# Modulation vectors of a two-layer adaLN trunk: four column groups by block of output features, and one transpose

## The reference

```python
def modulated_norm(x, g, shift, scale):
    return rmsnorm(x, g) * (1 + scale[:, None]) + shift[:, None]

def trunk_layer(x, c, lw, token_mix):
    ...
    mod = (jax.nn.silu(c) @ w_ada + b_ada).reshape(c.shape[0], N_SUB, 3, D_MODEL)
    x = half_ffn(x, mod[:, 0], g_norm[0], w_ff_up[0], w_ff_down[0])
    h = modulated_norm(x, g_norm[1], mod[:, 1, 0], mod[:, 1, 1])
    ...
    x = half_ffn(x, mod[:, 2], g_norm[2], w_ff_up[1], w_ff_down[1])
```

## Time and profile before

| | |
|---|---|
| time, median of 3 runs | 3243.67 us (3242.27 to 3249.42) |
| span of the profiled execution | 3248.1 us |
| PE busy | 3163.6 us, 97% of the span |
| PE weight loads busy | 2826.5 us, 87% |
| DVE busy | 1155.2 us, 36% |
| ACT busy | 827.2 us, 25% |
| granted clock of PE, mean | 0.984 |
| moved from HBM | 373.62 MB |

### The profile page before, as it was taken

One profiled execution on the slowest core, in us unless ns is written; L12 is line 12 of the kernel. 1 busy time (PEld: TensorE's weight loads), 2 busy tenths in 40 slices (PEclk: granted clock), 3 DMA queues, 4 the chain that ended last, 5 costly groups with the idle time before them and its releaser, 6 DMA issues.

```text
span 3248.1 us, 54636 instructions
## 1 busy us (share of the span) xinstructions
PE 3163.6 (97%) x23756; PEld 2826.5 (87%) x23756; DVE 1155.2 (36%) x1941; ACT 827.2 (25%) x1221; POOL 138.7 (4%) x269
## 2 busy tenths in 40 slices
PE   8999999999999999999999999999999999999999
PEld 6999998867777899999999999987676778899999
DVE  3332334235332334333343323342444223343333
ACT  3221224232331122212222212242323211222121
POOL 0000000000411000000000000000003120000000
PEclk9999999989999999999999999998999999999999
DMA  5444432111258432333223444312022583322212
GB/s 241 145 173 154 157 131 88 66 39 49 82 172 273 135 118 83 136 146 110 89 75 134 165 169 146 129 53 91 27 75 63 189 275 99 127 79 85 96 71 77
DMA packets 118735, 390.85 MB, mean 120 GB/s; under 512 B 12784, under 2 KB 63312, under 8 KB 100320
## 3 DMA queue, kind: packets, MB, share of 16 engines
q1 hardware_dynamic: 100464, 338.36, 29.2%
q0 software_dynamic: 14432, 34.09, 3.1%
q10 hardware_dynamic: 3600, 14.91, 1.2%
HBM read 373.62 MB, written 13.69 MB: 119 GB/s over the span
## 4 chain that ended last, share of the span: by engine, by line
PE 87%; DMA 4%; DVE 3%; ACT 3%; issue 1%; SPq 1%; ACTq 0%; DVEq 0%
PE g L839 78%; PE q L839 5%; PE tb L839 4%; DMA w<-in_w_up 2%; DMA area<-in_w_ada 1%; ACT area L1749 1%; DMA area<-in_cache_v 1%; DVE w_lo L1949 1%; ACT area L1755 0%; SPq L703 0%; DVE w_rest L1907 0%; DVE area L2138 0%; ACT w_hi L1477 0%; DVE area L1876 0%; DMA area<-in_cache_k 0%
## 5 line engine op out<-in xcount | busy, mean ns | idle before, releaser
L839 PE MATMUL g<-h_hi,w_hi 128*128 128x272 f32 x2784 | 582.6, 290 | 16.9 <-ACT area L1486 9.7
L1477 ACT ACTIVATE w_hi<-w 128x1024 fp32r<-128x1024 f32 (+2 forms) x232 | 266.2, 1147 | 1259.5 <-PE g L839 939.0
L839 PE MATMUL g<-h_hi,w_lo 128*128 128x272 f32 x2784 | 577.6, 289 | 0.0
L839 PE MATMUL g<-h_lo,w_hi 128*128 128x272 f32 x2784 | 574.2, 287 | 0.0
L1949 DVE TENSOR_TENSOR w_lo<-w,w_hi 128x1024 fp32r<-128x1024 f32 (+2 forms) x232 | 309.9, 1336 | 512.7 <-ACT w_hi L1477 509.4
L839 PEld LDWEIGHTS g<-h_hi,w_hi 128*128 128x128 f32 x2784 | 438.4, 190 | 36.8 <-ACT area L1486 23.9
L839 PEld LDWEIGHTS g<-h_lo,w_hi 128*128 128x128 f32 x2784 | 437.3, 188 | 0.0
L839 PEld LDWEIGHTS g<-h_hi,w_lo 128*128 128x128 f32 x2784 | 436.6, 188 | 0.0
L839 PE MATMUL g<-h_hi,w_rest 128*128 128x272 f32 x1184 | 343.0, 292 | 0.0
L839 PE MATMUL g<-acts_hi,w_hi 128*128 128x272 f32 x1408 | 294.8, 290 | 0.0
L839 PE MATMUL g<-acts_hi,w_lo 128*128 128x272 f32 x1408 | 291.2, 288 | 0.0
(11 more groups left out here) (301 smaller groups left out, 4318.7 us busy)
## 6 DMA issues: line engine op xcount, KB each, us to landing
w<-in_w_up SPq DMA_DIRECT2D x44, 2048.0 KB, 7.9
w<-in_w_ada SPq DMA_DIRECT2D x32, 2048.0 KB, 7.7
w<-in_w_in SPq DMA_DIRECT2D x16, 2048.0 KB, 7.7
w<-in_w_down SPq DMA_DIRECT2D x16, 1536.0 KB, 6.5
w<-in_w_gate SPq DMA_DIRECT2D x48, 512.0 KB, 5.6
w<-in_w_down SPq DMA_DIRECT2D x16, 1280.0 KB, 5.5
area<-in_cache_k SPq DMA_DIRECT2D x72, 256.0 KB, 3.6
area<-in_cache_v SPq DMA_DIRECT2D x72, 256.0 KB, 4.3
```

The source lines that it names most:

```text
L839: return pe.matmul(o, a, b, start=start, stop=stop, skip_group_check=True, **kw)
L1477: ac.activation(WH[i % 2][:, 0:n], W[place][:, o:o + n], ACT.Copy).then_inc(s_wh, 1)
```

## The change

The four column groups take the four blocks of 128 output features, where they took blocks of the input. Each group sums over all eight `k` itself, and writes 128 columns. So a step issues 32 matmuls of 128 moving columns where it issued 8 of 512. The copy by ACT is 128 x 128. Rows are turned by one transpose of 128 x 128; the sum over groups and its constant `fold` fall away. DVE reads the first 9 of each 32 columns of `tb`.

```diff
-               seq_later=NS, fold=C, seq01=NS, own_seq=SEQS, new_mask=2 * NS, new_seq=2 * 4,
+               seq_later=NS, seq01=NS, own_seq=SEQS, new_mask=2 * NS, new_seq=2 * 4,
...
-        MR, _ = take(2, 4 * P, start=o_f + 6 * T)
-        CRAW, _ = take(KD, C, start=o_f + 6 * T + 8 * P)
+        MR, _ = take(2, P, start=o_f + 6 * T)
+        CRAW, _ = take(KD, C, start=o_f + 6 * T + 2 * P)
...
                 for k in range(KD):
-                    last = mm(Q[k % 4 * 32:k % 4 * 32 + 32, n % 2, :], COND[:, k, :], w[:, k * 512:(k + 1) * 512],
-                              k < 4, k >= 4)
+                    for j in range(4):
+                        o = k * 512 + j * P
+                        last = mm(Q[32 * j:32 * j + 32, n % 2, 0:P], COND[:, k, :], w[:, o:o + P], k == 0, k == KD - 1)
...
-                for b in range(4):
-                    last = mm(TB[:, n % 2, b * C:(b + 1) * C], MR[:, n % 2, b * P:(b + 1) * P], fold, True, True)
-                last.then_inc(s_feat, 1)
+                turn(TB[:, n % 2, 0:P], MR[:, n % 2, :], ident).then_inc(s_feat, 1)
...
-                ac.activation(MR[:, n % 2, :], Q[:, n % 2, :], ACT.Copy).then_inc(s_mr, 1)
+                ac.activation(MR[:, n % 2, :], Q[:, n % 2, 0:P], ACT.Copy).then_inc(s_mr, 1)
...
-                ve.tensor_tensor(MOD[:, at4, :], TB[:, n % 2, 0:4 * C].rearrange("p (b c) -> p b c", b=4),
+                ve.tensor_tensor(MOD[:, at4, :], TB[:, n % 2, 0:P].rearrange("p (b c) -> p b c", b=4)[:, :, 0:C],
```

More of the change, by code:

```diff
@@ L92, in constants @@
     same = t[:, None] // STEPS == t[None] // STEPS
-    put("fold", i[:, None] % 32 == np.arange(C)[None])
     put("seq_later", np.where(same & (t[None] >= t[:, None]), 0, -BIG))
@@ L431, in build @@
         RS, _ = take(T, start=o_f + 5 * T)
-        MR, _ = take(2, 4 * P, start=o_f + 6 * T)
-        CRAW, _ = take(KD, C, start=o_f + 6 * T + 8 * P)
-        assert o_f + 6 * T + 8 * P + KD * C <= AREA
+        MR, _ = take(2, P, start=o_f + 6 * T)
+        CRAW, _ = take(KD, C, start=o_f + 6 * T + 2 * P)
+        assert o_f + 6 * T + 2 * P + KD * C <= AREA
         o_yb = 4 * T
@@ L499, in build @@
         half_sums, half_spread = const("half_sums"), const("half_spread")
-        fold = const("fold")
         later, tril01 = const("later"), const("tril01")
```

## The result

The changed kernel takes 3221.09 us (median of 4 runs, 3219.11 to 3227.16) against 3246.55 us before in the same comparison: a ratio of 0.9931, 95% interval 0.9916 to 0.9946, so 22 us less, with 18 to 27 inside the interval. Two later comparisons of the same two kernels gave 0.9911 (0.9884 to 0.9938) and 0.9924 (0.9910 to 0.9937). The forecast was 25.5 us less.

What follows compares the result with a forecast made beforehand. PE, busy 97% of the span, was taken as the bound, so instructions leaving its queue shorten the kernel. The terms -25.0 + 1.0 - 1.5 = -25.5 us gave 3218 us from 3243.67, range 3211 to 3230.

Steps and rivals of the forecast that it cites:

- Part 1: Fold of 8 records becomes one transpose, 0.03 us for 0.81: saves 0.78 us a step, 25.0 us in 32 steps.
- Part 2: Row products, 8 matmuls of 512 columns become 32 of 128: 1.87 to 1.88 us for 1.86, 1.0 us more in all.
- The form with 32 records: Cached keys' multiplication, 32 columns stationary, 128 moving, four groups in turn: 1.01 us, the base for pricing 64 records.
- The slower rival: In the row products the added weight loads lie bare, 12 more rounds a step: +25 us, 3269 us; chance 0.03.
- The issue rival: PE's issue bounds the row products' 64 pairs: at 35 ns a pair -14 us, 3229; at 41 ns no gain; chance 0.05.
- the sum: Whole kernel: -25.0 for the transpose, +1.0 for row products, -1.5 at the start, together -25.5 us, median 3218 us.
- Part 3: ACT's copy shrinks to 128 columns, DVE reads 36 elements with another stride; both hidden behind a unit, costed at nothing.
- Part 4: Up steps: split weights come next, margin 0.4 us; their chain starts where unit 2 ends, so the fold's 0.78 stays gain.
- the waits of 5.4 us: PE's waits for split weights in all, before the change; forecast to stay near 5 us but might vanish or double.
- the tiles' place: All tiles behind the constants move 32 bytes down; with other step moments, may make the 5.4 us of waits vanish or double.
- Part 5: Kernel start: two folds behind the fourth `w_ada` block save 2 x 0.78, taken as 1.5 us, bounds 0 and 2.

Runs made afterwards that it cites:

- the early split: DVE's second split of each chunk moved ahead of the subtraction making `acts_lo`: on the changed kernel 3211.96 and 3212.74 us, on the kernel before ratio 0.9977.
- the late fold: The kernel before with the fold behind the third unit of an up step in place of the first: ratio 1.0001 (0.9990 to 1.0012).

## Why the prediction was right, step by step

**Part 1, the transpose.** Right to a hundredth of a microsecond. The line through groups of eight and two gave 0.03 us for one, and 32 of 32 took 0.025 to 0.029 us behind the first unit. The saving is 0.811 - 0.027 = 0.784 us a step, 25.1 us. It is not lost again in the unit behind: its 26th matmul starts 4.03 us behind the fold's start at 136.83, and 3.24 us behind the transpose's start in the same step of the changed kernel. The run with the transpose alone brought 22 us.

**Part 2, the row products.** 1.884 us where 1.88 was forecast, 0.030 us more a step, 1.0 us in all. The form with 32 records was the right neighbour, and the slope from the earlier trace rows carried it to 64. The slower rival falls: its rule would have laid the 48 added loads bare, and the run with the row products alone is 1 us above before, not 50. The Trainium skill, TensorE: Matmul & The Clock Gate, section The mechanism, ties the overlap of loads and matmuls to different row groups; here all groups use the same rows, and the trace disagrees: 64 loads pass within 1.88 us when neighbours in the queue belong to different column groups. The issue rival falls with the same rows: 64 pairs in 1.884 us are 29 ns a pair, as the sum asked. Part 3, ACT and DVE at nothing, holds with it: the run with the row products alone has ACT's shorter copy, and gains nothing by it.

**Part 4, what is late next.** The step was right in what it said of the chain: the fold's gain is there in every up step (the unit behind it starts 0.78 us earlier against the kernel before), and the runs with the early split and the late fold moved SP's issue and the waits as the chain asks. The mis-sized term is the landing. The prediction said that the waits of 5.4 us might vanish or double with the moment and the place at which weights land; in the view it used they became 8.6, 7.1 and 7.9 us in three profiles, and by excess 10.1, 8.4 and 9.4 in place of 6.1. That is 2 to 4 us given back. Of the two reasons it offered, the tiles' place, 32 bytes lower, is refuted by two runs. That steps begin at other moments is not needed: the kernel before with a longer program does the same work in the same order, and waits 9.4 us. The cause of the slower landing stays open (last section).

**Part 5, the start.** The first norm stands at 45.14 where it stood at 46.49, so 1.35 us in place of 1.5. DVE's and PE's timelines of the start:

```profile
37.94 1.95 PE L837 MATMUL q<-area,cond 128*32 128x128 f32 x64 [1.60 <-DMA area<-in_w_ada]
...
41.54 2.56 PE L837 MATMUL g<-cst 128*128 128x272 f32 x10 [0.36 <-DVE mod L1917]
...
42.72 2.36 DVE L1934 TENSOR_TENSOR w_lo<-w,w_hi 128x1024 fp32r<-128x1024 f32 x2 [1.01 <-ACT w_hi L1438]
45.14 0.75 DVE L1873 SCALAR_TENSOR_TENSOR area<-x,amp,tb 128x512 f32<-128x512 f32 x1
```

From the row products of the fourth block to the end of the wait for the bias it is 3.60 us (41.54 - 37.94) where it was 5.08 (42.89 - 37.81): 1.48 us less, as forecast. The fourth block came 0.13 us later in this execution, hence the 1.35. The cover behind it is gone: DVE's first split now waits for ACT, whose weights land when they land, and the norm begins right behind the split: the cover of 1.03 us is used up.

That the two profiles give nearly the forecast is in part luck, for the start of a kernel with the fold differs from execution to execution. PE's and DVE's timelines and the stretch from 30 to 38 us, in the kernel before with 32 unused bytes:

```profile
30.07 2.63 PE L840 MATMUL q<-area,cond 128*32 128x512 f32 x16 [2.61 <-DMA area<-in_w_ada]
...
41.05 1.92 PE L840 MATMUL q<-area,cond 128*32 128x512 f32 x16
...
49.73 0.75 DVE L1877 SCALAR_TENSOR_TENSOR area<-x,amp,tb 128x512 f32<-128x512 f32 x1 [1.03 <-PE tb L840]
```
```profile
30.00:38.00 8.00, 7.93 (x36) 3.70 (x40) 0.20 (x1) 0.60 (x1) 0.00 (x0) 0.57 1.02 427
```

And in the changed kernel again:

```profile
38.05 1.95 PE L837 MATMUL q<-area,cond 128*32 128x128 f32 x64
...
45.24 0.75 DVE L1873 SCALAR_TENSOR_TENSOR area<-x,amp,tb 128x512 f32<-128x512 f32 x1
```

With the 32 unused bytes PE waits 2.61 us for a block of `w_ada`. In the stretch behind that its granted clock is 0.57 in the mean, so for most of it at the lower level, 1.2 GHz, and PE comes to the fourth block only at 41.05, without a wait for it. In the changed kernel again the clock of the same stretch is 0.79, and the fourth block is still used at 38.05. So what is saved ahead of that block does not always go into the wait for it; it also makes up for a slow stretch. In the seven profiles with the transpose (the run with groups one after the other left out) the first norm stands at 45.10 to 45.30, in the six with the fold at 46.49 to 49.73, in the mean 2.9 us later. The forecast of 1.5 us rests on the earliest of these six starts.

**The sum.** -25.1 + 1.0 - 1.35 + (10.1 - 6.1) = -21.5 us by the first profile, and -25.1 + 1.0 - 1.35 + 2.3 = -23.2 by the second; with 2.9 for the start they are -23.0 and -24.7. The ratios of the three comparisons say 22, 29 and 25 us. The spans differ by 3248.1 - 3221.1 = 27.0 us; the rest of that lies in the mixer stages, where the change does nothing and where single executions differ: the kernel before with 32 unused bytes has a span of 3235.5 us. Differences between two spans of single executions are not to be trusted below some 10 us here; terms read from start to start are.

## What to carry to other kernels

Price a new form of matmul by the nearest form that already runs in the trace, from start to next start, and check that neighbours in the queue go to different column groups: the same 64 pairs cost 1.88 us in turn and 5.88 us in a row. When work leaves a busy engine, find where the chain of the next late thing starts: work ahead of that point is a full gain, work beside it is margin. And look at what the chain waits for in DVE's order; one operation moved behind the release of a buffer brought 6 us more here. And read a start from more than one profile before a term is taken from it: here it differed by 3 us.

## What the runs showed of the hardware

**A fetch of instructions delays a load.** The 2 MB loads of `in_w_up` at 92.55 and at 147.18 in the kernel before, from the view of DMA queues (queue, packets, MB, share; then the issue with its time to landing):

```profile
q1 hardware_dynamic: 144, 2.10, 67.9%
q8 instruction: 1, 0.02, 0.7%
...
w<-in_w_up SPq DMA_DIRECT2D x1, 2048.0 KB, 8.7
```
```profile
q1 hardware_dynamic: 144, 2.10, 76.3%
...
w<-in_w_up SPq DMA_DIRECT2D x1, 2048.0 KB, 7.8
```

The first has a 16 KB packet of instructions among its packets, the second has none. Counted over the loads of `in_w_up` that ran alone, by the end of their last packet: 22 without such a packet between 1.5 and 7.3 us behind the issue end after 7.36 us in the median, 17 with one after 8.32 us. The Trainium skill, Runtime: NRT & Kernel Launch, section Instruction fetch mechanics, says that an engine's program comes in blocks of 16 KiB over a DMA queue of its own and that the cost is mostly hidden; the 188 packets of 16 KB in this trace agree with the size. What the page does not speak of is a data transfer: here it ends about 1 us later. That holds for the four kernels with as many PE matmuls as before (0.86 to 0.96 us); in the others, whose loads are slower even without a fetch, it is 0.2 to 0.4 us, in the changed kernel 8.24 us with a fetch (15 loads) against 7.96 without (24).

**The same load takes 7.3 or 7.9 us, by program.** Loads without a fetch end, in the median, after 7.36, 7.32, 7.34 and 7.26 us in the four kernels with as many PE matmuls as before, after 7.96, 7.92, 7.86, 7.94, 7.96, 7.99 and 7.92 us in the seven profiles of kernels with the change's count, after 7.87 us in the kernel before lengthened by as many instructions, 7.72 us in the one with the transpose alone (504 fewer) and 7.51 us in the one with the row products alone (3456 more). The landing goes with the program, stays the same when the order of work or the tiles' place changes, and does not grow steadily with the count. In two slow loads of the changed kernel, one of the sixteen first packets took 2.0 and 2.5 us, where the longest of a load at 147.18 in the kernel before took 1.57. Over all loads without a fetch the longest first packet takes 2.03 us in the median in the changed kernel and 1.76 before; but the load at 338.97 in the kernel before has one of 2.00 and ends after 7.41, so it is a mark of slow loads and not shown to be their cause. What in the program decides it was not found.
